# Expert loop: the next step's first gate piece is split ahead of the hidden rows' parts, and the last steps' row copies move ahead of the last pieces

## The chip, the cores and the metric

The kernel runs on 1 core of one Trainium2 chip. The metric is the device time of one execution in microseconds. A core has TensorE (PE in the rows; PEld is its weight load), VectorE (DVE), ScalarE (ACT), GpSimd (POOL) and SyncE (SP), each with an instruction queue of its own that runs in order, and 16 DMA engines. Engines meet only at semaphores.

## The reference

One encoder layer over 256 + 1024 = 1280 tokens of width 1024: a mixer (pooling and mLSTM) with residual, then a mixture of experts with residual, then a final norm. The change touches the experts alone:

```python
def expert_block(args):                     # 128 rows of one expert; 32 experts, top 2 of 8 in the chosen group
    xb, eb = args
    hb = jax.nn.silu(jnp.matmul(xb, w_gate[eb])) * jnp.matmul(xb, w_up[eb])   # 1024 -> 512, twice
    return jnp.matmul(hb, w_down[eb])                                          # 512 -> 1024
...
y = jax.ops.segment_sum(yrows[dest] * swt[:, None].astype(yrows.dtype), stok, num_segments=T)
```

## The kernel before, in words

The mixer, the norms and the router take the first 560 us or so. Then comes the expert stage: 32 steps here, one for each expert, numbered 0 to 31. Steps 0 to 3 are written out, the rest run in a loop of two steps a turn (`Fori(2, n_half)`, buffers b = 0 and b = 1), whose count each engine reads from `half_steps` into a register after step 3.

A matrix product of two float32 operands is made from three matmuls (`product3`, lines 938 to 943): each operand x is split into a rounded part x_hi (float32r) and the rest x_lo, and hi*hi, hi*lo and lo*hi are added in PSUM. Three kinds of operand are split this way:

- **Weights, in pieces.** A step streams 12 pieces of 512 KB through `e_st` (12 slots): eight of gate and up (`gu_piece(i, 0..7)`) and four of down (`down_piece(i, 0..3)`, which hold the down weights of expert i - 1). SP loads a piece (`piece_in`, L678) once the piece 12 before it has been split (`elo_done`). ScalarE copies it to `e_hi` (`hi_part`, L1509), VectorE subtracts to get `e_lo` (`lo_part`, L1982). `e_hi` and `e_lo` are rings of 6 pieces, so `hi_part` of a piece waits until TensorE has used the piece 6 before it (`piece_used`).
- **The expert's rows** (`gx`, gathered by GpSimd), turned by TensorE into PSUM (`ex_transposes`, L1196), then `ex_hi` (L1543) and `ex_lo` (L2022).
- **The inner rows** h = silu(gate) * up (`sg` L1561 on ScalarE, `hh` L2039 on VectorE), turned by TensorE (`h_turn`, L1230), then `ht_hi` (L1549) and `ht_lo` (L2027).

In step i TensorE does, in order: `gate_up(i)`, 8 pieces of 6 matmuls; the 8 transposes of the rows of step i + 1; the down product of step i - 1, 4 pieces of 6 matmuls, with the 4 transposes of `h_turn(i)` after its second piece. ScalarE and VectorE split pieces 0, 1, 2 of the step, copy half of the output rows of step i - 2 out of PSUM each (`y_half`, to `yo`, L1556 and L2033, which waits for the end of the down product of step i - 2), split pieces 3 to 7 and the four down pieces, then make `sg` and `hh`, the two `ex` parts for the next step, and last the `ht` part, which waits for `h_turn(i)`. GpSimd then sends `yo` to DRAM by a scatter.

After the last step (`last_i` = 31) four pieces are left, the down weights of expert 31 (`last_piece`). Their product may only write PSUM once the rows of step 30 have been copied out by both engines. Then the rows are read back, added to the residual, normed and stored.

Of the kernel before, what the change touches and what calls it, by code (L numbers as in the profile page):

```python
# [21 lines left out]
def build(nc, x_prompt, x_sample, norm1_g, w_in, pool_w, pool_scale, gate_b, head_norm_g, w_out,  # L22
# [236 lines left out]
    with ctx:  # L259
# [94 lines left out]
        N_FIRST = 2 * (NG - 1)  # L354

        last_use = {m: n + 1 for n, (_, m, _) in enumerate(proj)}
        parts_after = {}
        for m in range(NSL - 4):
# [37 lines left out]
        def unit(n):  # L396
            step, d = n // 2, n % 2
            return step, d, chunk_of(step, d)
# [62 lines left out]
        def wait(eng, s, value):  # L461

            if not isinstance(value, int) or value >= 1:
                eng.wait_ge(s, value)
# [5 lines left out]
        def outs_before(i, b):  # L470

            return 8 * i - 8 * b
# [24 lines left out]
        def gu_piece(i, c):  # L497
            if isinstance(i, int) and i == 0:
                return c, c, c % NRG, 1
            return 12 * i - 4 + c, (8 + c) % NST, (2 + c) % NRG, i + c // 4  # L500

        def down_piece(i, c):

            return 12 * i + 4 + c, 4 + c, (4 + c) % NRG, i + 1

        def last_piece(i, c):

            return 12 * i + 8 + c, 8 + c, (2 + c) % NRG, i + 1
# [782 lines left out]
        def _(act):  # L1291
# [172 lines left out]
            for n in range(NU):  # L1464
                step, d, ck = unit(n)
# [14 lines left out]
                i = wo_at.get(n)  # L1480
# [24 lines left out]
            def hi_part(piece):  # L1505
                number, slot, r, loads = piece
                act.wait_ge(e_load[slot], 16 * loads)
                wait(act, piece_used, number - NRG + 1)
                act.activation(e_hi[:, r, :, :], e_st[:, slot, :, :], ACT.Copy).then_inc(ehi_done, 1)  # L1509
# [30 lines left out]
            def ex_hi_part(i, b):  # L1540
                for half in range(2):
                    act.wait_ge(ext_ready, 2 * i + 1 + half)
                    act.activation(ex_hi[:, b, 4 * half:4 * half + 4, :],  # L1543
                                   psum[:, 2 + half, :].rearrange("p (k n) -> p k n", k=4),
                                   ACT.Copy).then_inc(exhi_done, 1)

            def ht_hi_part(i, b):
                act.wait_ge(ht_ready, i + 1)
                act.activation(ht_hi[:, b, :, :], psum[:, 6, :].rearrange("p (k n) -> p k n", k=KF),  # L1549
                               ACT.Copy).then_inc(hthi_done, 1)  # L1550

            def y_half(i, b, whole):

                act.wait_ge(piece_used, whole)
                wait(act, y_out[b], outs_before(i, b))
                act.activation(yo[:, b, 0:512], psum[:, 4, :], ACT.Copy).then_inc(y_left, 1)  # L1556

            def silu(i):
                act.wait_ge(piece_used, gu_piece(i, 7)[0] + 1)
                wait(act, h_ready, i)  # L1560
                act.activation(sg[:, :], psum[:, 0, :], ACT.Silu).then_inc(sg_done, 1)  # L1561

            def step(i, b, split=0):

                for c in range(split, 2):
                    hi_part(gu_piece(i, c))
                if not split:
                    hi_part(gu_piece(i, 2))
                if not isinstance(i, int) or i >= 2:
                    y_half(i - 2, b, down_piece(i - 1, 3)[0] + 1)  # L1570
                for c in range(max(split, 3), 8):
                    hi_part(gu_piece(i, c))
                for c in range(4):
                    hi_part(down_piece(i, c))
                silu(i)
                ex_hi_part(i + 1, 1 - b)
                ht_hi_part(i, b)

            for c in range(4, 6):
# [6 lines left out]
            silu(0)  # L1586
            ex_hi_part(1, 1)
            ht_hi_part(0, 0)
            step(1, 1, split=4)
            step(2, 0)  # L1590
            step(3, 1)
            n_half = load_half_steps(act)
# [1 line left out]
                step(2 * j, 0)  # L1594
                step(2 * j + 1, 1)
            last_i = 2 * n_half - 1
            for c in range(4):
                hi_part(last_piece(last_i, c))
                if c == 0:
                    y_half(last_i - 1, 0, down_piece(last_i, 3)[0] + 1)  # L1600
            y_half(last_i, 1, last_piece(last_i, 3)[0] + 1)


# [16 lines left out]
        def _(dve):  # L1620
# [262 lines left out]
            for n in range(NU):  # L1883
# [3 lines left out]
                i = wo_at.get(n - 1)  # L1887
# [91 lines left out]
            def lo_part(piece):  # L1979
                number, slot, r, _ = piece  # L1980
                dve.wait_ge(ehi_done, number + 1)
                dve.tensor_tensor(e_lo[:, r, :, :], e_st[:, slot, :, :], e_hi[:, r, :, :].bitcast(F32),  # L1982
                                  ALU.subtract).then_inc(elo_done, 1)
# [34 lines left out]
            def ex_lo_part(i, b):  # L2018
                for half in range(2):
                    k = slice(4 * half, 4 * half + 4)  # L2020
                    dve.wait_ge(exhi_done, 2 * i + 1 + half)
                    dve.tensor_tensor(ex_lo[:, b, k, :], psum[:, 2 + half, :].rearrange("p (k n) -> p k n", k=4),  # L2022
                                      ex_hi[:, b, k, :].bitcast(F32), ALU.subtract).then_inc(exlo_done, 1)

            def ht_lo_part(i, b):
                dve.wait_ge(hthi_done, i + 1)
                dve.tensor_tensor(ht_lo[:, b, :, :], psum[:, 6, :].rearrange("p (k n) -> p k n", k=KF),  # L2027
                                  ht_hi[:, b, :, :].bitcast(F32), ALU.subtract).then_inc(htlo_done, 1)

            def y_half(i, b, whole):  # L2030
                dve.wait_ge(piece_used, whole)
                wait(dve, y_out[b], outs_before(i, b))
                dve.tensor_copy(yo[:, b, 512:1024], psum[:, 5, :]).then_inc(y_right, 1)  # L2033
# [5 lines left out]
                dve.scalar_tensor_tensor(out=hh[:, :], in0=psum[:, 1, :], scalar=w_row[:, b:b + 1], in1=sg[:, :],  # L2039
                                         op0=ALU.mult, op1=ALU.mult).then_inc(h_ready, 1)  # L2040

            def step(i, b, split=0):

                for c in range(split, 2):
                    lo_part(gu_piece(i, c))
                if not split:
                    lo_part(gu_piece(i, 2))
                if not isinstance(i, int) or i >= 2:
                    y_half(i - 2, b, down_piece(i - 1, 3)[0] + 1)
                for c in range(max(split, 3), 8):  # L2050
                    lo_part(gu_piece(i, c))
                for c in range(4):
                    lo_part(down_piece(i, c))
                hidden(i, b)
                ex_lo_part(i + 1, 1 - b)
                ht_lo_part(i, b)

            dve.wait_ge(wexp_done, 1)
# [24 lines left out]
            hidden(0, 0)  # L2083
            ex_lo_part(1, 1)
            ht_lo_part(0, 0)
            step(1, 1, split=4)
            step(2, 0)
            step(3, 1)
            n_half = load_half_steps(dve)
# [1 line left out]
                step(2 * j, 0)  # L2091
                step(2 * j + 1, 1)
            last_i = 2 * n_half - 1
            for c in range(4):
                lo_part(last_piece(last_i, c))
                if c == 0:
                    y_half(last_i - 1, 0, down_piece(last_i, 3)[0] + 1)
            y_half(last_i, 1, last_piece(last_i, 3)[0] + 1)


# [54 lines left out]
```

## Time and profile before

| what | value |
|---|---|
| median of 3 runs | 1193.73 us (1190.48 to 1194.3) |
| span of the profiled execution, first to last instruction | 1184.8 us |
| median of the runs less that span | 8.9 us |
| granted TensorE clock, mean | 0.996 |
| TensorE matmul / weight load busy | 97% / 81% of the span |
| VectorE / ScalarE / GpSimd busy | 73% / 58% / 22% |
| moved by DMA | 324.12 MB, mean 274 GB/s |

The profiled execution has a span and no time of its own beside it; what lies around the span is taken as the 8.9 us by which the median of the runs exceeds it. Busy shares are averages over stages with different limits. A busy matmul row holds modelled ends, so gaps on TensorE are better read from the start times of its matmuls, which follow each other at a fixed distance when nothing is waited for.

### The profile page before, as it was taken

The numbers are of one execution on the slowest core, as the hardware profiler recorded it, in microseconds if no ns is written. First come the engines' busy times: TensorE is split into PE (matmuls) and PEld (weight loads), VectorE is DVE, ScalarE is ACT, GpSimd is POOL, SyncE is SP. The second block draws the span as 40 slices with busy tenths as digits, with TensorE's granted clock in tenths as the row PEclk, the third lists the DMA queues.
The fourth block names the chain that finished last, engine by engine and source line by source line (L and its number), as shares of the span: only waits on it lengthen the run. The fifth ranks groups of instructions, "written<-read, shape, count | busy, mean of one in ns | idle before, by whom it ended". The sixth has DMA issues, their size and how long they took to land.

```text
span 1184.8 us, 18749 instructions
## 1 busy us (share of the span) xinstructions
PE 1152.3 (97%) x5938; PEld 962.3 (81%) x5938; DVE 863.9 (73%) x1378; ACT 682.1 (58%) x1129; POOL 257.7 (22%) x354
## 2 busy tenths in 40 slices
PE   8999999999999899998999999999999999999997
PEld 8988888888889788876777888888888888888873
DVE  6649510235448657777798999999999999999976
ACT  6341231224348544313787787877877878778744
POOL 2200210001100012233141332323323323233230
PEclk9999999999999999999999999999999999999999
DMA  7312240446979535444999999999999999999999
GB/s 225 84 40 83 88 130 1 126 169 227 318 253 366 168 120 175 143 167 144 386 391 387 390 380 394 378 389 385 370 387 376 382 388 371 387 376 382 380 283 354
DMA packets 136900, 324.12 MB, mean 274 GB/s; under 512 B 24630, under 2 KB 61408, under 8 KB 136848
## 3 DMA queue, kind: packets, MB, share of 16 engines
q1 hardware_dynamic: 119136, 279.18, 64.5%
q0 software_dynamic: 17712, 44.27, 10.3%
q8 instruction: 30, 0.49, 0.2%
q14 instruction: 22, 0.18, 0.1%
HBM read 285.37 MB, written 51.12 MB: 284 GB/s over the span
## 4 chain that ended last, share of the span: by engine, by line
PE 82%; DVE 6%; DMA 5%; ACT 4%; issue 2%; SPq 0%; ACTq 0%; POOL 0%; POOLq 0%; DVEq 0%
PE psum L941 24%; PE psum L943 23%; PE psum L942 23%; DVE e_lo L1982 3%; ACT e_hi L1509 3%; PE psum L1196 2%; PE psum L1230 1%; PE psum L1124 1%; PE psum L955 1%; PE psum L1112 1%; DMA units<-mlstm_units 1%; PE psum L1274 1%; PE psum L987 1%; PE psum L1066 1%; PE psum L1072 1%
## 5 line engine op out<-in xcount | busy, mean ns | idle before, releaser
L1982 DVE TENSOR_TENSOR e_lo<-e_st,e_hi 128x1024 fp32r<-128x1024 f32 x384 | 442.5, 1218 | 13.3 <-ACT e_hi L1509 13.1
L1509 ACT ACTIVATE e_hi<-e_st 128x1024 fp32r<-128x1024 f32 x384 | 372.2, 1053 | 14.3 <-DMA e_st<-in_expert_w_gate_dram 7.2
L941 PE MATMUL psum<-e_hi,ex_hi 128*128 128x512 f32 x512 | 203.0, 397 | 5.3 <-DVE e_lo L1982 1.1
L943 PE MATMUL psum<-e_hi,ex_lo 128*128 128x512 f32 x512 | 200.0, 391 | 0.0
L942 PE MATMUL psum<-e_lo,ex_hi 128*128 128x512 f32 x512 | 199.6, 390 | 0.0
L941 PE MATMUL psum<-xT_hi,w_hi 128*128 128x512 f32 (+1 forms) x432 | 151.2, 350 | 2.2 <-DVE w_lo L1631 1.4
L943 PE MATMUL psum<-xT_hi,w_lo 128*128 128x512 f32 (+1 forms) x432 | 149.4, 346 | 0.0
L942 PE MATMUL psum<-xT_lo,w_hi 128*128 128x512 f32 (+1 forms) x432 | 149.2, 345 | 0.0
L941 PEld LDWEIGHTS psum<-e_hi,ex_hi 128*128 128x128 f32 x512 | 96.0, 188 | 37.8 <-DVE e_lo L1982 16.4
L943 PEld LDWEIGHTS psum<-e_hi,ex_lo 128*128 128x128 f32 x512 | 96.1, 188 | 20.5
L942 PEld LDWEIGHTS psum<-e_lo,ex_hi 128*128 128x128 f32 x512 | 96.2, 188 | 19.0
L941 PE MATMUL psum<-e_hi,ht_hi 128*128 128x512 f32 x256 | 105.7, 413 | 1.3 <-DVE yo L2033 1.1
L943 PE MATMUL psum<-e_hi,ht_lo 128*128 128x512 f32 x256 | 100.4, 392 | 0.0
L942 PE MATMUL psum<-e_lo,ht_hi 128*128 128x512 f32 x256 | 100.0, 391 | 0.0
L862 POOL COPY row_to<-rows_to 128x1 int32 (+1 forms) x30 | 28.4, 947 | 327.1 <-DVE yo L2033 327.1
L941 PEld LDWEIGHTS psum<-xT_hi,w_hi 128*128 128x128 f32 x432 | 82.3, 190 | 12.4 <-DVE w_lo L1631 1.6
L1631 DVE TENSOR_TENSOR w_lo<-w_st,w_hi 128x1024 fp32r<-128x1024 f32 x21 | 25.6, 1223 | 89.5 <-ACT w_hi L1304 89.4
L942 PEld LDWEIGHTS psum<-xT_lo,w_hi 128*128 128x128 f32 x432 | 82.3, 191 | 9.7
L943 PEld LDWEIGHTS psum<-xT_hi,w_lo 128*128 128x128 f32 x432 | 82.1, 190 | 10.0
L941 PE MATMUL psum<-wo_hi,mix_hi 128*128 128x512 f32 x160 | 64.8, 405 | 3.1 <-DVE mix_lo L1879 3.1
L1549 ACT ACTIVATE ht_hi<-psum 128x512 fp32r<-128x512 f32 x32 | 19.2, 601 | 78.6 <-PE psum L1230 78.6
L943 PE MATMUL psum<-wo_hi,mix_lo 128*128 128x512 f32 x160 | 63.2, 395 | 0.0
(281 smaller groups left out, 1913.2 us busy)
## 6 DMA issues: line engine op xcount, KB each, us to landing
e_st<-in_expert_w_gate_dram SPq DMA_DIRECT2D x128, 512.0 KB, 6.6
e_st<-in_expert_w_up_dram SPq DMA_DIRECT2D x128, 512.0 KB, 7.2
e_st<-in_expert_w_down_dram SPq DMA_DIRECT2D x128, 512.0 KB, 9.0
mlstm_units<-stage SPq DMA_DIRECT2D x18, 640.0 KB, 3.8
w_st<-in_w_in_dram SPq DMA_DIRECT2D x20, 512.0 KB, 4.4
xn_scratch<-xn POOLq DMA_DIRECT2D x20, 512.0 KB, 3.9
stage<-gate_rows SPq DMA_DIRECT2D x18, 512.0 KB, 5.9
e_st<-expert_rows SPq DMA_DIRECT2D x15, 512.0 KB, 9.1
```

What stands on the lines that cost most here:

```text
L862: pool.tensor_copy(row_to[:, b:b + 1], rows_to[:, bass.ds(i, 1)]).then_inc(row_placed, 1)
L941: pe.matmul(out, a_hi, b_hi, start=start, stop=False)
L942: pe.matmul(out, a_hi, b_lo, start=False, stop=False)
L943: return pe.matmul(out, a_lo, b_hi, start=False, stop=stop)
L955: last = pe.transpose(psum[:, 4 + 2 * (t % 2) + k // 4, (k % 4) * P:(k % 4 + 1) * P], xn[:, t % 2, k:D:KD], ident[:, :])
L987: last = pe.matmul(out[:, col:col + m], wpool[:, g, :], u_ext[:, g, first:first + m], start=True, stop=True)
L1066: pe.matmul(out, unit_part(n, H + h), state[:, d, h, :], start=True, stop=False)
L1196: last = pe.transpose(psum[:, 2 + half, (k % 4) * P:(k % 4 + 1) * P], gx[:, b, k:D:KD], ident[:, :])
L1509: act.activation(e_hi[:, r, :, :], e_st[:, slot, :, :], ACT.Copy).then_inc(ehi_done, 1)
L1549: act.activation(ht_hi[:, b, :, :], psum[:, 6, :].rearrange("p (k n) -> p k n", k=KF), ACT.Copy).then_inc(hthi_done, 1)
L1631: dve.tensor_tensor(w_lo[:, m % 4, :, :], w_st[:, m % 2, :, :], w_hi[:, m % 4, :, :].bitcast(F32), ALU.subtract).then_inc(wlo_done, 1)
L1982: dve.tensor_tensor(e_lo[:, r, :, :], e_st[:, slot, :, :], e_hi[:, r, :, :].bitcast(F32), ALU.subtract).then_inc(elo_done, 1)
```

## The change

Four edits, the same two on ScalarE (hi) and VectorE (lo). In `step(i, b)` the first piece of step i + 1 is split at the end of step i, between the `ex` part and the `ht` part; the step itself therefore begins at piece 1. `gu_piece(last_i + 1, 0)` is the same piece, slot and ring place as `last_piece(last_i, 0)`, so after the last step only last pieces 1 to 3 are left to split, and `y_half(last_i - 1)` now stands ahead of them. TensorE, SP and GpSimd programs are the same; no instruction is added or removed.

```diff
-            def step(i, b, split=0):
+            def step(i, b, first=1):
-                for c in range(split, 2):
+                for c in range(first, 3):
                     hi_part(gu_piece(i, c))
-                if not split:
-                    hi_part(gu_piece(i, 2))
                 if not isinstance(i, int) or i >= 2:
                     y_half(i - 2, b, down_piece(i - 1, 3)[0] + 1)
-                for c in range(max(split, 3), 8):
+                for c in range(max(first, 3), 8):
                     hi_part(gu_piece(i, c))
                 for c in range(4):
                     hi_part(down_piece(i, c))
                 silu(i)
                 ex_hi_part(i + 1, 1 - b)
+                hi_part(gu_piece(i + 1, 0))
                 ht_hi_part(i, b)
...
-            step(1, 1, split=4)
+            step(1, 1, first=4)
...
             last_i = 2 * n_half - 1
-            for c in range(4):
+            y_half(last_i - 1, 0, down_piece(last_i, 3)[0] + 1)
+            for c in range(1, 4):
                 hi_part(last_piece(last_i, c))
-                if c == 0:
-                    y_half(last_i - 1, 0, down_piece(last_i, 3)[0] + 1)
             y_half(last_i, 1, last_piece(last_i, 3)[0] + 1)
```

VectorE's program has the same edit with `lo_part`, `hidden`, `ex_lo_part` and `ht_lo_part` in the places of `hi_part`, `silu`, `ex_hi_part` and `ht_hi_part`.

## Rows read from the trace of the kernel before

**Rows 1.** The page's head.
```profile
span 1184.8 us, 18749 instructions
```
**Rows 2.** Groups of instructions, 500 to 1140 us: count, busy, mean, idle before.
```profile
L941 PEld LDWEIGHTS psum<-e_hi,ex_hi 128*128 128x128 f32 x512 | 96.0, 188 | 37.8 <-DVE e_lo L1982 16.4 <-issue 1.3 <-DVE ex_lo L2022 0.6
...
L2039 DVE SCALAR_TENSOR_TENSOR hh<-psum,w_row,sg 128x512 f32<-128x512 f32 x32 | 23.7, 742 | 0.8 <-ACT sg L1561 0.7
```
**Rows 3.** The chain that ended last, around 812 us: start, us, what.
```profile
809.01 0.49 PE psum L1230 x4
...
810.02 1.06 ACT e_hi L1509
```
**Rows 4.** Timeline of PE around the same step boundary.
```profile
811.62 0.39 PE L942 MATMUL psum<-e_lo,ht_hi 128*128 128x512 f32 x1
811.85 0.39 PE L943 MATMUL psum<-e_hi,ht_lo 128*128 128x512 f32 x1
812.38 0.50 PE L941 MATMUL psum<-e_hi,ex_hi 128*128 128x512 f32 x1
812.72 0.40 PE L942 MATMUL psum<-e_lo,ex_hi 128*128 128x512 f32 x1
```
**Rows 5.** Timeline of PE at the first boundary and at the loop's entry.
```profile
592.60 0.39 PE L943 MATMUL psum<-e_hi,ht_lo 128*128 128x512 f32 x1
593.22 0.47 PE L941 MATMUL psum<-e_hi,ex_hi 128*128 128x512 f32 x1 [0.24 <-DVE e_lo L1982]
593.53 0.39 PE L942 MATMUL psum<-e_lo,ex_hi 128*128 128x512 f32 x1
...
629.14 0.39 PE L943 MATMUL psum<-e_hi,ht_lo 128*128 128x512 f32 x1
630.20 0.50 PE L941 MATMUL psum<-e_hi,ex_hi 128*128 128x512 f32 x1 [0.67 <-DVE e_lo L1982]
630.53 0.40 PE L942 MATMUL psum<-e_lo,ex_hi 128*128 128x512 f32 x1
```
**Rows 6.** Timeline of ACT, 805 to 814 us.
```profile
805.90 1.08 ACT L1543 ACTIVATE ex_hi<-psum 128x512 fp32r<-128x512 f32 x2
809.52 0.60 ACT L1549 ACTIVATE ht_hi<-psum 128x512 fp32r<-128x512 f32 x1 [2.54 <-PE psum L1230]
...
813.34 8.64 ACT L1509 ACTIVATE e_hi<-e_st 128x1024 fp32r<-128x1024 f32 x9
```
**Rows 7.** Timeline of DVE, 807 to 815 us.
```profile
807.78 1.27 DVE L2022 TENSOR_TENSOR ex_lo<-psum,ex_hi 128x512 fp32r<-128x512 f32 x2
810.16 0.69 DVE L2027 TENSOR_TENSOR ht_lo<-psum,ht_hi 128x512 fp32r<-128x512 f32 x1 [1.10 <-ACT ht_hi L1549]
811.10 3.50 DVE L1982 TENSOR_TENSOR e_lo<-e_st,e_hi 128x1024 fp32r<-128x1024 f32 x3 [0.26 <-ACT e_hi L1509]
```
**Rows 8.** Single steps: length, PE, PEld, DVE, ACT, POOL busy, clock, DMA share, GB/s.
```profile
593.22:611.50 18.28, 18.04 (x85) 14.82 (x85) 16.95 (x18) 14.14 (x18) 7.98 (x5) 1.00 1.03 405
630.20:648.41 18.21, 18.06 (x85) 14.81 (x85) 16.86 (x18) 14.03 (x18) 5.42 (x5) 1.00 0.99 375
```
**Rows 9.** Weight loads (L678), issue to landing, in the steps at 593.22 and 757.74.
```profile
DMA to landing us min/median/max: 9.4/11.9/12.9
...
DMA to landing us min/median/max: 5.8/8.1/9.6
```
**Rows 10.** Timeline of SP, the four down loads of one step.
```profile
804.26 3.44 SPq L678 DMA_DIRECT2D e_st<-in_expert_w_down_dram  x4
```
**Rows 11.** TensorE's loop branch ahead of the boundary at 812.38.
```profile
L1247 PEldq COMPARE_BRANCH  x1: 215/215/215, 808.5 to 808.5; - x1
```
**Rows 12.** The last pieces: ACT, then DVE, then PE.
```profile
1140.35 0.60 ACT L1556 ACTIVATE yo<-psum 128x512 f32<-128x512 f32 x1 [1.29 <-PE psum L943]
...
1140.36 0.69 DVE L2033 COPY yo<-psum 128x512 f32<-128x512 f32 x1
...
1141.29 0.49 PE L941 MATMUL psum<-e_hi,ht_hi 128*128 128x512 f32 x1 [1.06 <-DVE yo L2033]
```

More of the change, by code:

```diff
@@ L2040, in hidden, with step @@
                                          op0=ALU.mult, op1=ALU.mult).then_inc(h_ready, 1)
-            def step(i, b, split=0):
-                for c in range(split, 2):
+            def step(i, b, first=1):
+                for c in range(first, 3):
                     lo_part(gu_piece(i, c))
-                if not split:
-                    lo_part(gu_piece(i, 2))
                 if not isinstance(i, int) or i >= 2:
                     y_half(i - 2, b, down_piece(i - 1, 3)[0] + 1)
-                for c in range(max(split, 3), 8):
+                for c in range(max(first, 3), 8):
                     lo_part(gu_piece(i, c))
@@ L2055, in step @@
                 ex_lo_part(i + 1, 1 - b)
+                lo_part(gu_piece(i + 1, 0))
                 ht_lo_part(i, b)
@@ L2085, in _ @@
             ht_lo_part(0, 0)
-            step(1, 1, split=4)
+            step(1, 1, first=4)
             step(2, 0)
@@ L2093, in _ @@
             last_i = 2 * n_half - 1
-            for c in range(4):
+            y_half(last_i - 1, 0, down_piece(last_i, 3)[0] + 1)
+            for c in range(1, 4):
                 lo_part(last_piece(last_i, c))
-                if c == 0:
-                    y_half(last_i - 1, 0, down_piece(last_i, 3)[0] + 1)
             y_half(last_i, 1, last_piece(last_i, 3)[0] + 1)
```

## The prediction

> **What bounds the kernel now.** I read the groups of instructions first: they say which wait TensorE has in the expert stage. Its weight loads at the first matmul kind of gate and up sat idle 16.4 us in all for `e_lo` of VectorE, the largest wait named there, and `hh` runs 32 times, so there are 32 steps and 30 boundaries from one `gate_up` to the next, into steps 2 to 31 [rows 2]. Next, the chain that ended last shows what such a boundary is: transposes of the inner rows, `ht_hi`, then the split of the first gate piece on ScalarE (810.02) and on VectorE (from 811.10), and only then TensorE's first matmul of `gate_up` at 812.38 [rows 3, 4, 7]. So the first piece is late because both engines stand before it waiting for `h_turn`, which has nothing to do with it. ScalarE has idled 2.54 us there and VectorE 1.10 us [rows 6, 7]. Last, the table of single steps gives the other engines' room: a step takes 18.21 us, VectorE is busy 16.86 of it, ScalarE 14.03, and the DMA engines' share is about 1.0 [rows 8]. TensorE sets the pace but for the gap, VectorE is 1.35 us behind it, and the DMA is the resource to worry about.
>
> **What the gap costs.** Matmuls of 512 columns start 0.23 us apart when nothing is waited for, as from 811.62 to 811.85. At the boundary the next starts are 812.38 and 812.72 [rows 4]: 0.53 and 0.34, together 0.87 where 0.46 would do. That is 0.41 us, of which 0.30 is the gap and 0.11 a slower first matmul after it. The boundary into step 2 shows 0.62 + 0.31, or 0.47 lost (that into step 3 looks the same), and the one at the loop's entry, where the engines also read the loop count, 1.06 + 0.33, or 0.93 lost [rows 5]. Sum over 30 boundaries: 27 x 0.41 + 2 x 0.47 + 0.93 = 12.9 us. If the slow first matmul stays (0.11 each, 3.3 us) the sum is 9.6. Nearest row for that: the first down matmul after the row transposes is slow too, without a wait, but it follows another kind of instruction, and `gate_up` follows matmuls of its own kind; so I take 12.9.
>
> **The edit inside the step.** The hi split of the next piece 0 now starts when the `ex` part is done: 805.90 + 1.08 = 806.98, ends 808.0, while `ht_hi` cannot start before 809.52 [rows 6]. It costs ScalarE nothing: the 2.54 us of idle time cover its 1.06 us. If that cover were gone, `ht_hi` would be late by up to 1.06 us; its reader is the down product of the next step, 11 us later. On VectorE `ex_lo` ends at about 809.0, the lo split takes 1.15 to 1.24 us and ends near 810.25, against 810.16 for `ht_lo` now [rows 7]: `ht_lo` is some 0.1 us late, and again nobody needs it for 11 us. What follows are pieces 1 and 2, and they come earlier than now. With time zero at TensorE's start of `gate_up` (812.08 in this step if it doesn't wait), ScalarE starts `ht_hi` at -2.6 and ends piece 1 at -1.0, VectorE ends that piece 1.24 us later at +0.25, then 1.14 us for each piece ((3.50 - 1.22) / 2 [rows 7]): piece 2 at +1.4, the row copy at +2.0, piece 3 at +3.1, piece 4 at +4.3. TensorE wants a piece every 6 x 0.228 = 1.37 us: +1.37, +2.73, +4.10, +5.46. The least margin is 1.0 us. Nothing else on that path moves: `hh` ends nine pieces and its own 0.74 us after the row copy, at +13.0, and `h_turn` wants it after ten pieces and the row transposes, 10 x 1.37 + 0.8 = +14.5. ScalarE's row copy, which used to come after piece 2 at 812.86, now waits for the end of the down product until about +0.3; that is 0.4 us of new idle time on an engine with 4 us to spare. The new step is 18.21 - 0.41 = 17.80 us, and VectorE's 16.86 fit in it.
>
> **The loop's branch.** It lies at every second boundary on TensorE's own queue and takes 0.215 us, so 14 x 0.215 = 3.0 us could appear once the gap doesn't hide it. The row shows it at 808.5, 3.9 us ahead of the matmul behind it [rows 11, 4]: the sequencer runs ahead while matmuls are in flight. I take 0; 3.0 is the bound.
>
> **The edit at the end.** In the last step both row copies start at 1140.35, when the down product of step 30 has ended, and TensorE goes on at 1141.29 behind VectorE's [rows 12]. In the new order the same two copies wait for the same end. VectorE's split of last piece 0 ended at 1140.33 and so was just out of the way before. Pieces 1 to 3 follow the copies in both. I take 0; the bound is 0.1 either way. The order of the piece and the copy matters only if the load of that piece were late, and it isn't.
>
> **Does the DMA keep up?** The split frees its slot earlier in the step and asks for its load earlier; the number of loads is the same. The time from issue to landing is the backlog. It falls from 9.4 to 12.9 us in the step at 593.22 to 5.8 to 9.6 in the step nine later [rows 9], so in that stretch the DMA works faster than it is asked: nine steps took 18.28 + 18.70 + 7 x 18.21 = 164.5 us, and the backlog fell by 3.3 to 3.6 us, so nine steps' transfers need about 161 us, 17.9 us a step. Against a step of 17.80 us the backlog would not fall but grow, by 0.1 us a step, 3 us over 29 steps, to about 16 us for the longest landing. What a late load may cost: the last down load of a step is issued at 804.26 + 3.2 = 807.4 [rows 10], and its hi split is the last of nine from 813.34 [rows 6] in the next step, 821.0, so 13.6 us later; VectorE reaches that piece 1.5 us after ScalarE has ended it, and TensorE bears at least 1.1 us beyond that before it waits (the margins above). That makes 16.2 to 16.5. So by these rows the DMA just about keeps up to the end of the loop. At 17.9 us a step the giveback is 0; at 18.0 it is 29 x 0.2 = 5.8 us of growth less 3.6 of room, 2.2 us. I take 0.5 us.
>
> A page of the Trainium skill, DMA: Bandwidth & Descriptors, section Bandwidth, gives 425 GB/s as measured for one core alone on large transfers and about 358 for HBM-bound ones. A step moves about 7.0 MB (18.21 us at about 385 GB/s): 16.5 us by the first figure, with nothing given back (the sum is then 12.9), and 19.6 by the second, which would forbid this change any gain. The trace has held 405 GB/s for a whole step [rows 8], so the second is not a limit here; the first is above anything that a whole step shows.
>
> **Sum.** The profiled span is 1184.8 us [rows 1]; 1184.8 - 12.9 + 0.5 = 1172.4. With the 8.9 us that the median of the runs has over it: 1181.3 us, 1.04% under the median of 1193.73.
>
> **The rivals.**
> - *The DMA becomes the bound in mid-loop.* For it: its share is at 1.0 already, and the 17.9 is worked out from backlog alone. Against: the backlog falls now, and there is room. If the need is 18.0 us and only 2 us of room are real, the room is gone after 10 steps and then each saves 0.2: 10 x 0.41 + 20 x 0.21 + 0.6 = 8.9 us saved, about 1184.8. Chance 0.18.
> - *The first matmul's slowness or the branch stays.* 9.6 or 9.9 saved: about 1184. Chance 0.10.
> - *The wait is only renamed.* TensorE has piece 0, but waits as long for piece 1 or `ex_lo`, or the edit doesn't move the split because ScalarE's ring place isn't free yet. Against: margins of 1.0 us, and the ring needs gate piece 6 of the step to be used, which is so 3 us before. 1193.7, chance 0.06.
> - *Slower: the early split waits for its load.* `hi_part` of the next piece 0 now stands ahead of `ht_hi`, pieces 1 and 2 and the row copy in ScalarE's queue, and VectorE hangs behind. Its load must land within 14.7 us of its issue; it takes 9.4 down to 5.8 us, the least of each step, which is this piece [rows 9]. It decides from 14.7 + 1.1 us of slack + 0.42 of gap saved, some 16.2 us. At 17 us from issue to landing every boundary would cost 0.8 us more than now: 30 x 0.8 = 24, so 1218. Only the loads of the very first steps are slow enough, so a lasting wait is unlikely. Chance 0.04.
>
> **How the numbers follow.** My forecast has 0.62; its own range is 1178.5 to 1183.5 (the medians of the runs spread by 0.3%). The cases at 1184 to 1185 add 0.28. The range that holds 8 in 10 or more reaches from 1177.5 to 1187.0. About 0.3% (3.6 us) is what a measurement here can tell from no change. The first two cases and the forecast are all faster by more: 0.90. Same: 0.06. Slower: 0.04.
>
> **What the profile of the changed kernel would show.** Right: steps of about 17.80 us with starts 0.23 us apart through the boundary; the wait of `gate_up` for `e_lo` gone from 16 us to near 0; `ht_hi` still waiting about 1.5 us for `h_turn`; VectorE busy 16.86 of 17.80; an unchanged stretch from the last boundary to the end. Landings should stop falling and stay near 10 to 13 us, or rise. Wrong: waits of `e_hi` for DMA late in the loop (first rival), a start 0.3 us late behind each boundary or only each second one (second), a new wait for piece 1 (third), `e_hi` at piece 0 waiting for `e_st` (fourth).

## The result, and the profile after

The changed kernel took 1181.59 us (median of 4 runs, 1178.82 to 1185.29) against 1194.01 for the kernel before (4 runs, 1190.48 to 1195.49): ratio 0.990, 95% interval 0.9873 to 0.9927. The median is 0.3 us from the forecast. The profile shows that three terms of the sum were wrong by more than that; how the hit came about is told below.

**The boundary.** Timeline of TensorE after, around one step boundary (start, us, instruction), against [rows 4]:

```profile
645.86 0.39 PE L942 MATMUL psum<-e_lo,ht_hi 128*128 128x512 f32 x1
646.08 0.39 PE L943 MATMUL psum<-e_hi,ht_lo 128*128 128x512 f32 x1
646.31 0.39 PE L941 MATMUL psum<-e_hi,ex_hi 128*128 128x512 f32 x1
646.53 0.39 PE L942 MATMUL psum<-e_lo,ex_hi 128*128 128x512 f32 x1
```

The gap is gone and the first matmul behind it takes 0.39 us, not 0.50. The starts lie 0.22 to 0.23 us apart all the way. The old gap also made the matmuls behind it a little slower: from the first start of a step to the seventh, 1.50 us before and 1.35 after (timeline of TensorE, before and then after).

```profile
939.94 0.50 PE L941 MATMUL psum<-e_hi,ex_hi 128*128 128x512 f32 x1
...
941.44 0.39 PE L941 MATMUL psum<-e_hi,ex_hi 128*128 128x512 f32 x1
```

```profile
681.82 0.39 PE L941 MATMUL psum<-e_hi,ex_hi 128*128 128x512 f32 x1
...
683.17 0.39 PE L941 MATMUL psum<-e_hi,ex_hi 128*128 128x512 f32 x1
```

**The steps.** The table of single steps after, with the columns of [rows 8]:

```profile
593.05:610.80 17.75, 17.75 (x85) 14.89 (x84) 16.94 (x18) 14.28 (x17) 7.99 (x5) 1.00 1.03 406
646.31:664.06 17.75, 17.75 (x85) 14.89 (x84) 16.86 (x18) 14.50 (x17) 5.44 (x5) 1.00 1.02 402
842.10:860.66 18.56, 18.03 (x85) 14.81 (x84) 16.90 (x18) 14.92 (x17) 5.64 (x5) 1.00 1.02 406
```

An unhindered step takes 17.75 us instead of 18.21. TensorE is busy for all of it, and VectorE's work is what it was. But the third row is a longer one. There are six such steps between 742 and 1110 us: 18.20 at 806, 18.56 at 842, 18.20 at 1003 and three of 17.87.

**The loads.** Issue to landing of a step's weight loads after, in the steps at 593 and at 1020, against [rows 9]:

```profile
DMA to landing us min/median/max: 11.3/13.6/14.6
...
DMA to landing us min/median/max: 13.2/14.4/15.8
```

Before, they fell to 4.6/7.4/8.7 by the end of the loop. After, they rise at first (13.7/14.9/15.5 at 753) and then stay: in the steps between 735 and 1092 us the longest landing of a step lies between 15.1 and 16.6 us. The table of waits between 500 and 1130 us (us in all, times, longest) shows what this costs ScalarE, which before the change waits for no load in the loop:

```profile
ACT e_hi L1509 <- DMA e_st<-in_expert_w_down_dram: 43.6, 82, 1.6
ACT ht_hi L1549 <- PE psum L1230: 31.2, 32, 1.6
```

Most of these 82 waits cost the kernel nothing. This is one that does, in the step of 18.56 us (timeline of ScalarE, then VectorE, then TensorE; the time in brackets is the idle time before the instruction):

```profile
854.29 1.06 ACT L1509 ACTIVATE e_hi<-e_st 128x1024 fp32r<-128x1024 f32 x1 [1.34 <-DMA e_st<-in_expert_w_down_dram]
...
855.38 1.22 DVE L1980 TENSOR_TENSOR e_lo<-e_st,e_hi 128x1024 fp32r<-128x1024 f32 x1 [1.18 <-ACT e_hi L1509]
856.52 0.74 DVE L2037 SCALAR_TENSOR_TENSOR hh<-psum,w_row,sg 128x512 f32<-128x512 f32 x1
...
857.32 0.75 PE L1230 MATMUL psum<-ident,hh 128*128 128x128 f32 x4 [0.53 <-DVE hh L2037]
```

Read it downwards. The last down load lands 1.34 us after ScalarE asks for it, VectorE then idles 1.18 us, and TensorE waits 0.53 us for `hh`, which stands behind that piece in VectorE's queue. The transposes that need it start 15.22 us into this step instead of 14.53, and the slower matmuls behind the wait bring the loss to the 0.81 us that the step is longer. So the late load is not missed at its own piece but at the inner rows, which have 1.5 us of margin by the prediction (13.0 against 14.5).

**The end.** From the start of `gate_up` of step 31 to the end of the kernel before took 62.65 us, and after takes 67.02. Timeline of TensorE, among the last pieces, first one line of before that stands behind those of [rows 12], then after:

```profile
1143.21 0.50 PE L941 MATMUL psum<-e_hi,ht_hi 128*128 128x512 f32 x1 [0.27 <-DVE e_lo L1982]
```

```profile
1129.05 0.49 PE L941 MATMUL psum<-e_hi,ht_hi 128*128 128x512 f32 x1 [1.06 <-DVE yo L2031]
...
1130.96 0.50 PE L941 MATMUL psum<-e_hi,ht_hi 128*128 128x512 f32 x1 [0.27 <-DVE e_lo L1980]
...
1136.65 0.50 PE L941 MATMUL psum<-e_hi,ht_hi 128*128 128x512 f32 x1 [2.46 <-DVE e_lo L1980]
```

The wait for the row copy, 1.06 us, and that of 0.27 us for a piece are the same as before. New is the wait of 2.46 us before the last piece. Ahead of it ScalarE idles 3.06 us before its hi split at 1134.28. The profile puts that down to TensorE, which had long been done; what came last is the load, issued at 1113.8. The last loads took up to 20.1 us from issue to landing. GpSimd issues five accumulating DMAs (`x<-expert_rows`, which add rows in DRAM to the residual) at 1117.90, while they are under way; e8 and e9 below show that it matters. The last product ended 28.50 us after step 31's start (read from the start of VectorE's row copy behind it), against 25.57 before; the last scatter then took 7.15 us to land against 6.40, and the first row loads behind it 7.83 against 7.19.

**The books.** The profiled span after is 1177.1 us, 7.7 less than [rows 1]. It divides by the starts of `gate_up`:

| stretch | before | after |
|---|---|---|
| first instruction to step 1 | 574.95 | 575.19 |
| step 1 to 2 | 18.27 | 17.86 |
| step 2 to 31 | 528.93 | 517.03 |
| step 31 to the end | 62.65 | 67.02 |

With the cleanest loop measured (514.85 us, run e2 below) as the one with no late load, the boundaries are worth 528.93 - 514.85 + 0.4 = 14.5 us. Late loads take back 517.03 - 514.85 = 2.2 us in the loop and the end 4.4 us, and 0.2 lie ahead of step 1: 14.5 - 2.2 - 4.4 - 0.2 = 7.7.

### The profile page after: what moved, and what is told of

It is laid out like the page before. It is cut to its first block, busy times and chain, and to the rows that moved or that the text cites. A ratio compares the mean times of both kernels' runs of the same rounds, so it can differ in the third digit from the quotient of the medians.

```text
span 1177.1 us, 18748 instructions
## 1 busy us (share of the span) xinstructions
PE 1145.8 (97%) x5938; PEld 964.8 (82%) x5938; DVE 865.0 (73%) x1378; ACT 699.5 (59%) x1129; POOL 283.2 (24%) x354
## 4 chain that ended last, share of the span: by engine, by line
PE 59%; DMA 27%; DVE 7%; ACT 3%; issue 2%; SPq 1%; POOL 0%; ACTq 0%; DVEq 0%; POOLq 0%
DMA e_st<-in_expert_w_down_dram 21%; PE psum L941 16%; PE psum L943 16%; PE psum L942 16%; DVE e_lo L1980 3%; ACT e_hi L1509 2%; PE psum L1124 1%; DMA e_st<-in_expert_w_gate_dram 1%; PE psum L1196 1%; PE psum L955 1%; PE psum L1112 1%; DMA units<-mlstm_units 1%; PE psum L1274 1%; PE psum L987 1%; PE psum L1066 1%
## 5 line engine op out<-in xcount | busy, mean ns | idle before, releaser
L1980 DVE TENSOR_TENSOR e_lo<-e_st,e_hi 128x1024 fp32r<-128x1024 f32 x384 | 448.5, 1218 | 30.6 <-ACT e_hi L1509 29.5
L1509 ACT ACTIVATE e_hi<-e_st 128x1024 fp32r<-128x1024 f32 x384 | 392.9, 1057 | 69.8 <-DMA e_st<-in_expert_w_down_dram 44.1
L941 PE MATMUL psum<-e_hi,ex_hi 128*128 128x512 f32 x512 | 199.4, 389 | 0.3 <-DVE ex_lo L2020 0.3
L862 POOL COPY row_to<-rows_to 128x1 int32 (+1 forms) x30 | 52.3, 1744 | 290.2 <-DVE yo L2031 290.2
L942 PE MATMUL psum<-wo_lo,mix_hi 128*128 128x512 f32 x160 | 63.0, 394 | 0.0
## 6 DMA issues: line engine op xcount, KB each, us to landing
e_st<-in_expert_w_down_dram SPq DMA_DIRECT2D x128, 512.0 KB, 14.9
```

What stands on the lines that cost most here:

```text
L862: pool.tensor_copy(row_to[:, b:b + 1], rows_to[:, bass.ds(i, 1)]).then_inc(row_placed, 1)
L941: pe.matmul(out, a_hi, b_hi, start=start, stop=False)
L942: pe.matmul(out, a_hi, b_lo, start=False, stop=False)
```

## The experiments

The kernel before was measured again beside each group: 1190.15 us (13 runs) for e1 to e4, 1191.40 (15 runs) for e5 to e8 and 1192.93 (11 runs) for e9 to e12. The ratios are against these runs. A stretch or a wait of an experiment is read from one profiled execution of it.

### e1 and e2: half the bytes in the down loads, without and with the change

```diff
-                sp.dma_start(dst if d2 else dst.rearrange("p a n -> p (a n)"), src).then_inc(e_load[slot], 16)
+                sp.dma_start(dst if d2 else dst[:, 0:1, :], src).then_inc(e_load[slot], 16)
...
-                         .rearrange("a (p k) n -> p (a k) n", k=KF)[:, c, :], False)
+                         .rearrange("a (p k) n -> p (a k) n", k=KF)[:, c:c + 1, 0:512], 0)
```

The computation changes: half of each down piece isn't loaded, and what the slot held is used in its place. Every instruction of the engines is the same.

> The kernel before, but each of the down pieces loads only its first 512 of 1024 columns (the rest of the slot keeps old data, so the expert outputs are not the reference's): 1.05 MB less for each step of about 7.0 MB. Theory (in the kernel before the DMA is not the bound): steps stay at 18.21 us, landings fall to some 5 us early in the loop, time within 4 us of before (a shorter end possible, since the last four loads are halved). Rival (the DMA already holds back the kernel before in its unprofiled executions, which are 8 us longer than the profiled one): 1184 to 1188 us.

> The changed kernel with the same halved down loads. Theory (the change gives 12.9 us and the late transfers take back 2 us in the loop and 4 us behind it): every step 17.75 us, no wait of ScalarE for the DMA after step 3, the stretch from the start of step 31 to the end back to 62.7 us or less, time 1175 to 1178 us, 12 to 14 us under e1. Rival (the longer end comes from the new order of row copy and pieces): end stays at 66 to 67 us and the time at 1180.

Measured: e1 1190.02 us (1186.35 to 1193.48), ratio 0.9998 (0.9982 to 1.0014). So the kernel before is not bound by its transfers. e2 1173.93 us (1171.33 to 1176.25), ratio 0.9866 (0.9842 to 0.9889). A step of e2 late in the loop, in the table of single steps:

```profile
808.02:825.77 17.75, 17.75 (x85) 14.89 (x84) 16.86 (x18) 14.15 (x17) 5.43 (x5) 1.00 0.92 328
```

All its steps take 17.75 us, and the end takes 61.37 us. The time is 1.1 us below the range expected for it. With room in the DMA the change is worth 16.1 us by the medians (1190.02 - 1173.93), with the real loads 12.4. The boundaries explain 14.5 of the 16.1; the profile of e1 also has two longer steps at the start of the stage (19.82 and 19.23 us into steps 2 and 3, where e5 below has 18.25 each), and how common those are is not known.

### e3 and e4: 256 KB more to move in each step, without and with the change

SP issues one more DMA, from DRAM to DRAM, behind the down loads of each step of the loop:

```diff
+                sp.dma_start(units_dram.rearrange("t b p j h n -> (t b p) (j h n)")
+                             .rearrange("(e r) n -> e r n", e=E)[bass.ds(expert_at(i), 1), 0:64, 0:1024],
+                             expert_w_down[0, bass.ds(expert_at(i), 1), 0:64, :]).then_inc(extra, 16)
```

> The kernel before with one more transfer for each step: SP copies 256 KB of a weight matrix to a DRAM scratch that nobody reads any more. By the backlog, a step's transfers then need 17.9 x 7.2 / 6.95 = 18.6 us against 18.21: the backlog grows 0.36 us a step, the room of 3.6 us is gone after 10 steps, the rest is exposed: 6 to 10 us slower than before. Rival (the DMA has room to 425 GB/s): no change, 1194.

> The changed kernel with the same extra 256 KB for each step. Theory: steps settle at 18.6 us as in e3, since both kernels then go at the pace of the transfers; within 4 us of e3, so that nearly all of the change's gain is gone. Rival (the DMA has room): 1181 to 1183, 12 us under e3.

Measured: e3 1205.13 us (1204.8 to 1205.97), ratio 1.0125 (1.0108 to 1.0142); e4 1201.66 (1200.23 to 1203.48), ratio 1.0093 (1.0076 to 1.0109). The extra DMA costs the old order 15 us, where 6 to 10 were expected, and the change is then worth 3.5 us, as expected. A step of e3, and its waits between 560 and 1210 us:

```profile
780.92:799.75 18.83, 18.35 (x85) 14.73 (x85) 16.95 (x18) 14.72 (x18) 6.29 (x5) 1.00 1.02 391
```

```profile
ACT e_hi L1513 <- DMA e_st<-in_expert_w_down_dram: 52.5, 80, 3.1
```

The old order, too, now waits for down loads: from step 2 to 31 its steps take 18.68 us on average, and those of e4 18.51 (from 17.75 to 23.09 each, not settled at 18.6 as expected). Its end is 66.81 us, against 62.65 and 63.75 in the two profiles of the kernel before: a backlog is enough for a long end, and the new order of the copies isn't needed for it. e2 shows the other half: the new order with no backlog ends in 61.37 us.

### e5: the kernel before once more

> The kernel before, unchanged, for a second profile. Theory: the loop is the same as in the first profile (steps 18.21 to 18.24 us, 528.9 us from the start of step 2 to that of step 31, end 62.7 us); what makes its other executions longer than the profiled one lies ahead of step 2. Rival: some steps of the loop are longer and wait for the DMA. Time as before.

Measured: 1191.28 us (1187.74 to 1193.67), ratio 1.0004 (0.9988 to 1.002). Its profiled span is 1188.4 us, 3.6 more than [rows 1]: 2.5 lie ahead of step 1, 0 between steps 2 and 31 (528.93 in both) and 1.1 in the end, which was expected to stay. This execution took 1.7 us more than its span, as did every other whose own time is given beside the span. So the 8.9 us around the span were not there: the profiled execution of before was simply a short one.

### e6 and e7: ScalarE's half alone, VectorE's half alone

e6 is the changed kernel with VectorE's program put back (`lo_part` of piece 0 at the start of the step again), e7 with ScalarE's:

```diff
 # e6: VectorE; e7: the same lines with hi_part, on ScalarE
-            def step(i, b, first=1):
+            def step(i, b, split=0):
...
-                lo_part(gu_piece(i + 1, 0))
```

> ScalarE's program of the changed kernel with VectorE's of the kernel before: the hi split of the next piece 0 is early, the lo split still stands behind ht_lo. In the rows of before VectorE waited 0.26 us for ScalarE there; without that, its lo split ends at about 812.04 where TensorE would come at 812.08. Theory (both engines' order mattered, ScalarE's for the larger part): the gap of 0.30 us goes to 0 or 0.1, 9 to 13 us faster than before less what the transfers take back, 1181 to 1186. Rival (VectorE's own order is what holds TensorE): under 3 us faster.

> VectorE's program of the changed kernel with ScalarE's of before: VectorE waits for the hi split of the next piece 0, which comes behind ht_hi, and does ht_lo only then. Theory: piece 0 is not earlier (lo split still from 811.10), and ht_lo now stands between pieces 0 and 1, so that piece 1 ends near 814.0 where TensorE wants it at 813.75: the gap stays and a second small one may come, 0 to 9 us slower than before. Rival: faster by more than 3 us.

Measured: e6 1184.44 us (1183.09 to 1189.81), ratio 0.9943 (0.9922 to 0.9965); e7 1206.53 (1202.55 to 1209.53), ratio 1.0126 (1.0098 to 1.0153). The boundary of e6 on TensorE:

```profile
649.16 0.39 PE L943 MATMUL psum<-e_hi,ht_lo 128*128 128x512 f32 x1
649.39 0.46 PE L941 MATMUL psum<-e_hi,ex_hi 128*128 128x512 f32 x1
649.68 0.40 PE L942 MATMUL psum<-e_lo,ex_hi 128*128 128x512 f32 x1
```

ScalarE's edit alone takes away the 0.26 us that VectorE idled before its split [rows 7], and the gap with it. A slow first matmul stays (0.29 to the next start) and the step takes 17.84 to 17.89 us. The profile calls the gap a wait for `e_lo` of VectorE [rows 2], since that signal comes last; behind it stood ScalarE. e6 also stays in trouble with its loads: from 10.9/13.2/13.9 us in the step at 593 they rise to 13.6/15.4/15.8 in the step at 1009, and single steps take 19.19 and 19.39 us. (The profiled execution was the longest of its six, 1189.81 us.) e7, on VectorE and TensorE:

```profile
651.87 1.23 DVE L1982 TENSOR_TENSOR e_lo<-e_st,e_hi 128x1024 fp32r<-128x1024 f32 x1 [1.96 <-ACT e_hi L1509]
...
653.01 0.69 DVE L2027 TENSOR_TENSOR ht_lo<-psum,ht_hi 128x512 fp32r<-128x512 f32 x1
...
654.43 0.39 PE L943 MATMUL psum<-e_hi,ex_lo 128*128 128x512 f32 x1
654.88 0.50 PE L941 MATMUL psum<-e_hi,ex_hi 128*128 128x512 f32 x1
```

Here VectorE's split stands ahead of `ht_lo` and waits 1.96 us for a hi part that ScalarE makes only after `ht_hi`. `ht_lo` is then in the way of piece 1, and TensorE has its old gap and a second one of 0.45 us between starts: steps of 18.71 to 18.76. The mechanism is the expected one, its price is not: 15.1 us slower, where 0 to 9 were expected. VectorE's half alone is worse than none, and ScalarE's alone gives 7.0 us where both together give 10.7 to 12.4.

### e8: the accumulating DMAs behind the scatter of step 30

```diff
-            for t in range(N_ADDED):
-                add_rows(t)
...
+                if b == 0:
+                    for t in range(N_ADDED):
+                        add_rows(t)
```

> The changed kernel with GpSimd's five accumulating transfers (add_rows, 512 KB each), which it issues while the last weight pieces are still under way, put behind the scatter of step 30's rows, some 12 us later. Theory (the longer end is the last down pieces waiting behind other transfers): the last pieces land by 1129 to 1131 and TensorE ends the last product 2 to 4 us earlier; of that 0 to 3 us are left at the end, as the adds then meet the row loads: 1178 to 1181. Rival (the end is bound by something else): no change, or 2 to 4 us slower because the rows are added late.

Measured: 1182.94 us (1181.06 to 1188.94), ratio 0.995 (0.9922 to 0.9978). The last product now ends 25.4 us after step 31's start, 3 us earlier, and its last loads land within 12.7 us, not 20.1. By this alone it could also be that this execution had less of a backlog: its loop took 515.33 us, with few late loads. e9 below settles that. The time is above the 1178 to 1181 expected. The chain that ended last shows where the 3 us went (start, us, what):

```profile
1136.07 0.70 DVE yo L2032
...
1137.67 11.19 DMA expert_rows<-yo,row_to
```

The last scatter takes 11.19 us to land instead of 7.15, now that the accumulating DMAs lie beside it, and the end takes 68.68 us. The bytes have to pass somewhere.

### e9 to e12: the changed kernel again, and three attempts to go on from it

e9 is the changed kernel. e10 splits last piece 1 ahead of the row copies of step 30, on both engines. e11 is e10 with the load of the final norm's gain moved from behind the last down loads to ahead of the expert stage. e12 is the changed kernel without the gather of the routing weights, 128 values of 4 bytes a step; a plain load of 8 values stands in its place, so these weights are wrong.

```diff
 # e10 (ScalarE; the same with lo_part on VectorE)
-            y_half(last_i - 1, 0, down_piece(last_i, 3)[0] + 1)
             for c in range(1, 4):
                 hi_part(last_piece(last_i, c))
+                if c == 1:
+                    y_half(last_i - 1, 0, down_piece(last_i, 3)[0] + 1)
 # e11, beside that
             sp.wait_ge(x1root_done, NT)
+            sp.wait_ge(mixlo_done, NT)
+            sp.dma_start(gf_b[:, :], final_norm_g.rearrange("(a d) -> a d", a=1).broadcast_to([P, D])).then_inc(norms_in, 16)
 # e12
-                    rows = row_of[:, b:b + 1]
+                    pool.dma_start(w_row[0:8, b:b + 1], w_dram[0:8, :]).then_inc(factor_in[b], 16)
+                    return
```

> The changed kernel, unchanged, beside e10 to e12 on the same chip and for a second profile. Theory: steps of 17.75 us with a few longer ones, 515 to 519 us from step 2 to step 31, an end of 65 to 68 us, 9 to 13 us faster than before. Rival (the long steps and the long end belong to one execution only): 515 us and an end of 62 to 63.

> The changed kernel with its last edit turned back in kind: one of the last pieces (now last piece 1, as piece 0 is already split) is split ahead of the copies of step 30's rows. Both engines idle there for 2.2 and 1.5 us, so the piece fits in. Theory: the 0.42 us gap of TensorE ahead of piece 1 goes; the last piece's late load then decides anyway, so 0 to 0.4 us, same time as e9. Rival (the order of copies and pieces is what makes the end longer): end 2 us or more shorter than e9's.

> As e10, and the 512 KB load of the final norm's gain, now issued behind the last pieces, goes ahead of the expert stage, where the DMA is idle. It takes 1.3 us of transfers out of the end, in which they are what is late. Theory: end 0 to 2 us shorter than e10's, time 0 to 2 us under e9. Rival: no change, or a later start of the loop since the load now meets the first pieces.

> The changed kernel without the gather of the rows' routing weights in the loop (128 packets of 4 bytes a step): 8 words are loaded by a plain transfer in its place, so from step 4 on the expert outputs are scaled by zero or a wrong weight. It asks whether these packets cost transfer time. Theory (the DMA's time goes by packets as well as by bytes): 0.1 to 0.4 us less for each step's transfers, so no wait of ScalarE for the DMA late in the loop, 515 us from step 2 to 31 and an end of 62 to 65, 2 to 6 us under e9. Rival (bytes alone count): as e9.

| kernel | median us (range) | ratio (95%) | step 2 to 31 | end |
|---|---|---|---|---|
| e9 | 1182.22 (1180.45 to 1183.08) | 0.9914 (0.9893 to 0.9936) | 517.26 | 70.21 |
| e10 | 1182.35 (1177.92 to 1186.96) | 0.9911 (0.9887 to 0.9936) | 517.79 | 69.48 |
| e11 | 1180.62 (1178.26 to 1184.2) | 0.9909 (0.9884 to 0.9934) | 517.46 | 66.16 |
| e12 | 1180.98 (1176.98 to 1185.01) | 0.9906 (0.9881 to 0.9932) | 517.47 | 66.35 |

None can be told from the changed kernel. e9 confirms the result and the loop of 517 us; its end is longer than the 65 to 68 expected. e11 gives no gain clear of noise either.

**e10** moves nothing in the time, but its trace shows what the order of the piece and the copies is for. (This execution took 1186.96 us, the longest of its six.) Timeline of ScalarE, then TensorE:

```profile
1133.05 1.06 ACT L1509 ACTIVATE e_hi<-e_st 128x1024 fp32r<-128x1024 f32 x1 [1.53 <-DMA e_st<-in_expert_w_down_dram]
...
1136.20 0.79 PE L941 MATMUL psum<-e_hi,ht_hi 128*128 128x512 f32 x1 [2.57 <-DVE yo L2032]
```

The load of last piece 1 was late here, VectorE's row copy stood behind its split, and TensorE waited 2.57 us for the copy instead of 1.06. The next matmuls started 0.42 to 0.43 us apart, and the granted clock was 0.66 from 1135 to 1140. The last product ended 29.39 us after step 31's start. So with a backlog the order does matter: a copy that stands ahead of the piece, as in the change, can't be held up by its load. In e11, with the same order as e10, the piece came in time and the wait was 1.06 us.

**e12** was meant to take 120 small packets out of each step, and its loop and its waits for down loads are nearly those of the changed kernel: between 600 and 1120 us 38.9 us in 73 waits, against 40.3 in 77 in the first profile of the changed kernel and 36.4 in 73 in e9. The row of e12:

```profile
ACT e_hi L1510 <- DMA e_st<-in_expert_w_down_dram: 38.9, 73, 1.6
```

But e12 took out no packet that the profile counts. The packets of the whole execution in e9, then e12, then e2:

```profile
DMA packets 136900, 324.12 MB, mean 275 GB/s; under 512 B 24630, under 2 KB 61408, under 8 KB 136848
```

```profile
DMA packets 136900, 324.10 MB, mean 276 GB/s; under 512 B 24630, under 2 KB 61408, under 8 KB 136848
```

```profile
DMA packets 136900, 290.56 MB, mean 248 GB/s; under 512 B 24630, under 2 KB 61408, under 8 KB 136848
```

So e12 tests neither its theory nor the rival, and what small packets cost stays open. The comparison that counts is e2: as many packets, 1 MB of some 7 less in each step, and the loop is free.

The end of e9 is 3.2 us longer than that of the first profile, though its last product was done 25.39 us after step 31's start, 3 us earlier. GpSimd's timeline in e9, then VectorE's beside it:

```profile
1111.93 10.03 POOL L862 COPY row_to<-rows_to 128x1 int32 x1 [9.99 <-DVE yo L2031]
...
1122.84 1.01 POOL L865 DMA_INDIRECT expert_rows<-yo,row_to  x1 [0.88 <-POOL row_to L862]
...
1125.81 4.62 POOL L881 DMA_DIRECT2D x<-expert_rows  x5
...
1111.62 10.30 DVE L1980 TENSOR_TENSOR e_lo<-e_st,e_hi 128x1024 fp32r<-128x1024 f32 x9
```

A copy of 128 integers that ends in 0.95 us elsewhere took 10.03 us here. The scatter of step 29's rows and the five accumulating DMAs behind it in GpSimd's queue start 8.8 and 8.4 us later than in the first profile, and the last scatter then takes 11.98 us to land. Another 1.65 us lie behind the landing of the first row loads: from 1158.1 to 1161.1 the granted clock was 0.50 in e9 (TensorE had been busy 2.71 of the 6 us ahead), and 1.00 in the same place of the first profile (busy 4.86 of 6; table of windows, e9, then the first profile).

```profile
1158.10:1161.10 3.00, 3.00 (x4) 1.45 (x5) 2.93 (x6) 2.78 (x6) 0.00 (x0) 0.50 1.05 415
```

```profile
1157.00:1160.00 3.00, 2.95 (x7) 1.44 (x8) 2.93 (x6) 2.78 (x6) 0.00 (x0) 1.00 1.02 410
```

The ends side by side, in us. The accumulating DMAs and the last product are counted from step 31's start; the loads are the down loads issued behind that start, with their longest landing; the last column but one is what lies behind the landing of the first row load.

| profile | accumulating DMAs at | longest load | last product ends | last scatter lands in | rest | end |
|---|---|---|---|---|---|---|
| before | 8.26 | 5.1 | 25.57 | 6.40 | 20.05 | 62.65 |
| e7 | 8.85 | 7.4 | 26.04 | 8.55 | 21.80 | 67.58 |
| e3 | 8.26 | 19.3 | 28.00 | 7.54 | 20.18 | 66.81 |
| changed | 7.82 | 20.1 | 28.50 | 7.15 | 20.09 | 67.02 |
| e11 | 7.83 | 19.6 | 27.85 | 7.45 | 20.32 | 66.16 |
| e12 | 6.13 | 19.0 | 27.32 | 7.72 | 20.11 | 66.35 |
| e9 | 16.22 | 11.6 | 25.39 | 11.98 | 21.74 | 70.21 |
| e8 | 20.67 | 12.7 | 25.45 | 11.19 | 20.06 | 68.68 |

With a backlog at the end of the loop, the end has two ways to be long: the accumulating DMAs lie early and the last down loads are late, or they lie late and the last scatter is. e9, the changed kernel itself with a loop as in the first profile, shows that this is not an effect of e8's lighter loop. e7 shows that an end can be long without a backlog, too, by a longer scatter and by the rest, so the end isn't explained to the last us.

## Why the prediction was right, and where its sum was not

**The gap.** Right in kind, too small by 1.6 us: 14.5, not 12.9. It was the boundary that I read as 0.41 us [rows 4]; the step fell by 0.46, from 18.21 to 17.75. The four starts that I compared hold 0.41 of it: 0.30 of gap and 0.11 of slow first matmul. The rest, 0.04, lies in the next matmuls of the first piece, whose seven starts span 1.50 us before and 1.35 after.

**The rival that the slow first matmul or the branch stays: refuted.** The first matmul takes 0.39 us, and steps are 17.75 us whether a loop branch lies in them or not. e6 shows that the slowness is real where the weights come just in time: 0.46 us for the first matmul, and 0.29 to the next start, with no wait shown in its row.

**Margins of pieces 1 to 4, `ht_hi`, ScalarE's idle time: right.** No piece of gate or up is waited for by TensorE in an unhindered step. `ht_hi` still waits 1.6 us at most for `h_turn`. The rival of a renamed wait is refuted.

**The slower rival: refuted.** Piece 0 was never waited for long enough to stop a boundary, though the least landing of a step, that of this piece, rose to 13.9 us (in the step at 967; 13.7 in that at 753) where it had been 5.8 [rows 9]. That is 0.8 us short of the 14.7 at which this piece begins to be late, so the rival was nearer than its 0.04 says.

**Does the DMA keep up? The step that failed.** I took a giveback of 0.5 us; it was 6.6, and 4.4 of that in a place where I had written "unchanged". The level of the backlog was read well, its course was not. I had it grow from 12.9 to about 16 us over the whole loop; it stood at 14.6 in step 2 already, reached 16.1 by the step at 735, and then stayed between 15.1 and 16.6 until the last two steps, while single steps grew longer. The point where it costs time is where the sum put it, at 16.2 to 16.5: the three steps of 18.20 and 18.56 us follow steps whose longest landing was 16.6, 16.2 and 16.3. For the loop my other bound, 2.2 us, was the measured value, but it came from 18.0 us of transfers a step, and no run here measures that figure, so the match is luck in part. What I didn't follow is where the backlog goes when the loop ends. Before, the loads of the last steps land within 7.5 us when the five accumulating DMAs come, after within 14.9; the last down pieces are then late, and nothing comes behind them that could hide it. e3 makes the long end with the old order and more bytes, e2 makes a short one with the new order and fewer bytes, and e8 and e9 move the loss to the last scatter. In the second pair of profiles (e5 and e9) the end gives back 6.5 us, not 4.4.

The trace agrees with neither figure of the page DMA: Bandwidth & Descriptors of the Trainium skill (section Bandwidth) that the prediction weighed. That page of the Trainium skill gives 425 GB/s for one core alone and about 358 for each core when both cores of a memory domain stream, so the second isn't a figure for this kernel. By the first nothing would have been given back, by the second no gain would have been left; steps under a backlog hold 388 to 406 GB/s, and the gain is partly given back.

**The DMA as the bound in mid-loop (0.18): in part.** It is true that late loads appear there. But the loop as a whole kept 11.9 of 14.1 us. The DMA isn't the bound of most steps after, but it is close to it. In e4, with 256 KB more in each step, the loop takes 19.7 us longer, and the gain falls to 3.5 us.

**The end (0, bound 0.1): right for the edit, wrong for the place.** TensorE waits 1.06 us for VectorE's row copy as before. I wrote that the order of piece and copy matters only if the piece's load is late, "and it isn't". With the backlog of the changed kernel it can be: in e10, which has a piece ahead of the copy, TensorE waited 2.57 us.

**The sum.** By its own terms it should have read 1184.8 - 14.5 + 6.6 + 0.2 = 1177.1 for the span, 4.7 more than my 1172.4, and 1.7 around it, 1178.8. I had put 8.9 there. So the hit on the time rests on luck: a span that was too low and a surrounding that was too large. That surrounding stands for how short the profiled execution of before was. The medians differ by 12.4 us (10.7 in e9), the spans by 7.7 (8.6 from e5 to e9). Where the rest lies stays open: the runs without a profile have no trace, and the stretch before step 1 alone varies from 574.5 to 580.8 us among profiles.

## What to carry to other kernels

When an edit shortens a loop, compare the new step with the time that the step's transfers need, and read that from the trend of issue-to-landing times over several steps, not from the DMA's share, which was about 1.0 in the kernel before, with room, and in the changed one, without. Then follow the backlog past the last step: in the loop most late loads are hidden, at the end the last ones are not, and transfers that were harmless there with an empty queue are not with a full one. If two engines hand a tile on, move both halves of the step. Before the sum is made, ask whether the profiled execution is a typical one. And before an experiment is read, check in its trace that it took away what it was meant to take.

## What the runs showed of the hardware

**A small GpSimd copy can be held up for 10 us.** All 27 of GpSimd's copies `row_to<-rows_to` between 640 and 1130 us, before and then after (duration min/median/max in ns, first and last start in us):

```profile
L862 POOL COPY row_to<-rows_to x27: 932/947/951, 651.5 to 1125.2; 128x1 int32 x27
```

```profile
L862 POOL COPY row_to<-rows_to x27: 934/949/10021, 648.5 to 1112.7; 128x1 int32 x27
```

The longest one after, with VectorE's timeline beside it:

```profile
1059.26 10.02 POOL L862 COPY row_to<-rows_to 128x1 int32 x1 [10.67 <-DVE yo L2031]
...
1058.93 10.30 DVE L1980 TENSOR_TENSOR e_lo<-e_st,e_hi 128x1024 fp32r<-128x1024 f32 x9
```

It ends at 1069.28, with the end of nine back-to-back splits of VectorE (1069.23). Two more took 7.76 and 8.90 us (791.03, 898.43). e8 to e11 each show one of 10.02 or 10.03 us (e10 another of 7.76), and e4 four of 4.36 to 7.76. The profiles of before, e1, e2, e3, e5, e6, e7 and e12 show none. The Trainium skill, SBUF — State Buffer, says in its practical consequences that a VectorE instruction with two SBUF inputs, as these splits are, contends with a GpSimd instruction that reads SBUF. The trace fits that, and adds that the wait can last for a whole run of such instructions; that the port is the cause is read from the ends falling together, no run isolates it. What decides whether the copy is held up is open: before, the same copy starts beside nine such splits as well (1070.50, with the splits from 1070.18 for 10.29 us) and takes 0.94. In the loop nobody waits for the copy; at the end, as in e9, its 9 us delay the accumulating DMAs.

**The DMA's share says little of room.** Its column reads 1.03 in the step at 593 both before [rows 8] and after. In the step at 630 before, with landings about to fall, it reads 0.99, and in the steps after that are shown 1.02. In e2, which moves 328 GB/s in a step without a late load, it is still 0.92.
